# Expert pairs of a two-block transformer kernel: VectorE turns activations and places in 32x32 blocks, and three loads are issued at other times

## The chip, the cores and the metric

The kernel runs as one program on one core of one Trainium2 chip. The metric is the time of one execution on the device, in microseconds (us). The engines are PE (TensorE), DVE (VectorE), ACT (ScalarE), POOL (GpSimd) and SP (SyncE, which here only issues DMAs).

## The reference

Two transformer blocks run one after the other on 256 tokens of width 1024, all in fp32. The first has a convolution, a windowed attention and a gated delta rule side by side, then a hierarchical mixture of experts. The second has gated linear attention and block attention, then PEER, a lookup in tables of 16384 rows. The change is in the mixture of experts and in loads around it:

```python
pg = softmax(xt @ wg + bg); grp = argmax(pg)            # 4 groups of 8 experts
top_logit, top_e = top_k(el_grp, 2)                     # two experts of the group
gate = pg_top * softmax(top_logit)
...
def expert_block(args):
    xb, e = args
    return (silu(xb @ w1[e]) * (xb @ w3[e])) @ w2[e]    # w1, w3: 1024x512, w2: 512x1024
...
ys = ys * gate
return zeros_like(xt).at[tok].add(ys)
```

## The kernel before

**Expert weights.** The 32 experts are worked through in 16 pairs. A pair has six weight tiles of 2048 KB, which are two of w1, two of w3 and two of w2. All 96 tiles are read once, in this order, by DMAs that SP issues (`expert_tile`). Eight places hold them (`PLACES`): six slots of `ring` and two places called `beside`, each made of two halves of 1024 KB, three of the halves in `work` and one in `consts`. SP fills a place again when the semaphore `w_used` says that the matmuls on its old tile are over. PE raises `w_used` by two at the start of an "a" layer, a "b" layer and a gathering, so two places come free at each of these three points of a pair.

**A pair on PE.** Each expert takes at most 64 tokens (`CAP`), so the two experts of a pair share the 128 columns of PE's array. For pair p, PE runs:

- `first_layer(p, "a", 0)` (rows x w1) and `first_layer(p, "b", 2)` (rows x w3), 16 matmuls of 512 columns each
- `gathered(p + 1)`: the next pair's rows are picked out of `h_tok` with the 0/1 matrix `pm`
- "at": four PE transposes of `act_p` (silu(a)*b, rows by features), which DVE copies from PSUM to `actT`
- `scattered(p - 1)`: the last pair's result is added to its tokens through `pgT`
- "pt": two PE transposes of `pg`, the places times the gates, which DVE copies to `pgT`
- "y": `actT` x w2, in two halves of the width

**The order of banks.** `expert_jobs()` lists the PSUM results in the order in which PE makes them, with the engine that takes each. The class `Jobs` gives them the eight PSUM banks in turn, and a job waits until the result that lay in its bank before has been taken.

**Around the experts.** `na_out`, the output of the windowed attention, is in `work` at columns 15104 to 15615, inside the half `beside[0][1]` (13312 to 15359). So the four halves of the two `beside` tiles are issued after the matmuls "yT1" have read it. POOL loads `norm2_w`, the second block's second norm, into `mod[:, 0, :]` as the experts start. The first wait for a `w_used` in the loop over tiles stands here (`q` counts the tiles behind the first eight):

```python
with sp.Fori(0, 3) as i:
    for q in range(24):
        sp.wait_ge(w_used, i * 24 + (q + 3))
        expert_tile(i * 8 + (2 * ((8 + q) // 6) + q % 2), (8 + q) % 6, q % PLACES)
```

## Time and profile before

| | |
|---|---|
| three runs | 1512.1, 1512.28 and 1514.79 us, median 1512.28 |
| profiled execution, its span | 1512.7 us |
| PE busy | 1384.3 us, 92% |
| DVE busy | 788.9 us, 52% |
| ACT busy | 284.5 us, 19% |
| POOL busy | 325.9 us, 22% |
| moved by DMA | 551.35 MB, 364 GB/s on the mean |

The profile gives the profiled execution no other time than its span; it is 0.4 us above the median of the runs. Busy time of PE is time in which a matmul was under way, also when it was under way slowly. DMA share is the mean busy share of the 16 DMA engines, GB/s what they moved. In the timeline, the time in brackets behind a row is how long the engine sat idle before it, and what it waited for.

### The profile page before, as it was taken

The numbers are of one execution on the slowest core, as the hardware profiler recorded it, in microseconds if no ns is written. First come the engines' busy times: TensorE is split into PE (matmuls) and PEld (weight loads), VectorE is DVE, ScalarE is ACT, GpSimd is POOL, SyncE is SP. The second block draws the span as 40 slices with busy tenths as digits, with TensorE's granted clock in tenths as the row PEclk, the third lists the DMA queues.
The fourth block names the chain that finished last, engine by engine and source line by source line (L and its number), as shares of the span: only waits on it lengthen the run. The fifth ranks groups of instructions, "written<-read, shape, count | busy, mean of one in ns | idle before, by whom it ended". The sixth has DMA issues, their size and how long they took to land.

```text
span 1512.7 us, 16972 instructions
## 1 busy us (share of the span) xinstructions
PE 1384.3 (92%) x6354; PEld 721.6 (48%) x6354; DVE 788.9 (52%) x1912; ACT 284.5 (19%) x700; POOL 325.9 (22%) x315
## 2 busy tenths in 40 slices
PE   6999999999999999998999999997997877788787
PEld 4886665444444444443565755544453332333332
DVE  2257565232332332232534787757676666767555
ACT  1432313000000000000334433221212121212112
POOL 0001303000000000000000245444444443444451
PEclk9999999999999999999999999999999999998999
DMA  9743669999999999999343599999999999999997
GB/s 380 299 163 113 238 279 365 425 426 426 426 426 427 426 427 427 423 427 425 146 155 124 211 395 391 420 421 422 421 421 421 421 421 422 422 421 422 421 422 313
DMA packets 64579, 551.35 MB, mean 364 GB/s; under 512 B 9168, under 2 KB 9440, under 8 KB 11760
## 3 DMA queue, kind: packets, MB, share of 16 engines
q1 hardware_dynamic: 26080, 278.06, 44.5%
q0 software_dynamic: 38416, 272.17, 43.7%
q8 instruction: 53, 0.87, 0.2%
q14 instruction: 30, 0.25, 0.0%
HBM read 549.16 MB, written 1.05 MB: 364 GB/s over the span
## 4 chain that ended last, share of the span: by engine, by line
PE 62%; DMA 32%; issue 3%; DVE 1%; POOL 1%; ACT 1%; SPq 0%; POOLq 0%; DVEq 0%
DMA ring<-peer_uv_d,work 16%; PE ps L2051 12%; PE ps L1957 11%; PE ps L1299 7%; PE ps L2093 6%; DMA work<-peer_uv_d,work 5%; PE ps L1785 4%; DMA ring<-expert_w_d 4%; PE ps L1293 4%; PE ps L1746 3%; PE ps L2062 3%; PE ps L1614 2%; DMA consts_sb<-peer_uv_d,work 2%; DMA work<-expert_w_d 2%; DMA ring<-w_ada_d 2%
## 5 line engine op out<-in xcount | busy, mean ns | idle before, releaser
L1957 PE MATMUL ps<-ring,work 128*128 128x512 f32 x686 | 335.8, 631 | 73.0 <-ACT work L1230 71.8
L3281 DVE CUSTOM_DVE_ANT_0 ring<-ring,work 128x1024 f32<-128x1024 f32 x172 | 211.6, 1231 | 137.6 <-DMA ring<-peer_uv_d,work 136.3
L1957 PEld LDWEIGHTS ps<-ring,work 128*128 128x128 f32 x686 | 133.5, 201 | 253.7 <-issue 149.7
L2244 POOL DMA_INDIRECT ring<-peer_uv_d,work x170 | 187.9, 1105 | 231.3 <-PE ps L1957 206.5
L2051 PE MATMUL ps<-ring,work 128*64 128x512 f32 x768 | 168.1, 592 | 3.0 <-DMA ring<-expert_w_d 2.4
L1230 ACT ACTIVATE work<-consts_sb,work 128x128 f32<-128x128 f32 x256 | 85.2, 392 | 283.1 <-DVE work L3290 276.0
L1299 PE MATMUL ps<-ring,hT 128*128 128x512 f32 (+1 forms) x272 | 112.6, 569 | 1.8 <-DVE hT L3106 1.6
L2051 PEld LDWEIGHTS ps<-ring,work 128*64 128x64 f32 x768 | 57.0, 137 | 111.0 <-issue 111.0
L2824 DVE TENSOR_TENSOR work<-work,ps 128x512 f32<-128x512 f32 x16 | 11.0, 688 | 185.7 <-PE ps L2051 185.7
L2219 POOL DMA_DIRECT2D mod<-subkeys_d x1 | 0.5, 546 | 457.1 <-DVEq L2889 457.1
L1078 ACT ACTIVATE work<-ps 128x512 f32<-128x512 f32 x16 | 9.6, 597 | 430.6 <-PE ps L2051 430.6
L1957 PE MATMUL ps<-work 128*128 128x512 f32 x172 | 83.8, 614 | 4.6 <-ACT work L1230 4.6
L2093 PE MATMUL ps<-ring,work 128*64 128x512 f32 x384 | 85.0, 595 | 0.7 <-DVE work L2828 0.7
L1785 PEld LDWEIGHTS ps<-hT,ring 128*128 128x128 f32 x640 | 75.7, 192 | 13.0 <-issue 12.4
L1299 PEld LDWEIGHTS ps<-ring,hT 128*128 128x128 f32 x272 | 50.8, 190 | 56.5 <-issue 54.3
L1785 PE MATMUL ps<-hT,ring 128*128 128x128 f32 x640 | 76.5, 275 | 0.0
L2835 DVE TENSOR_TENSOR work<-ps,mod 128x512 f32<-128x512 f32 x32 | 22.1, 692 | 89.1 <-PE ps L2093 89.1
L3281 DVE CUSTOM_DVE_ANT_0 work<-work 128x1024 f32<-128x1024 f32 x43 | 52.7, 1225 | 27.4 <-DMA work<-peer_uv_d,work 27.1
L1746 PEld LDWEIGHTS ps<-work 128*128 128x128 f32 x512 | 58.4, 192 | 13.2 <-issue 13.2
L1957 PE MATMUL ps<-mod,work 128*128 128x512 f32 x80 | 43.8, 674 | 22.2 <-ACT work L1230 22.2
L1746 PE MATMUL ps<-work 128*128 128x128 f32 x512 | 61.4, 278 | 0.3 <-issue 0.3
L2062 PE MATMUL ps<-work 128*128 128x512 f32 x128 | 57.7, 593 | 0.8 <-DVE work L2835 0.8
(481 smaller groups left out, 1722.9 us busy)
## 6 DMA issues: line engine op xcount, KB each, us to landing
ring<-expert_w_d SPq DMA_DIRECT2D x72, 2048.0 KB, 19.3
work<-expert_w_d SPq DMA_DIRECT2D x36, 1024.0 KB, 18.6
ring<-w_ada_d SPq DMA_DIRECT2D x12, 2048.0 KB, 8.7
ring<-w_in_d SPq DMA_DIRECT2D x11, 2048.0 KB, 22.8
consts_sb<-expert_w_d SPq DMA_DIRECT2D x12, 1024.0 KB, 19.6
ring<-w_out_d SPq DMA_DIRECT2D x4, 2048.0 KB, 8.3
ring<-peer_w_query_d SPq DMA_DIRECT2D x4, 2048.0 KB, 7.7
ring<-w_in_d SPq DMA_DIRECT2D x4, 1024.0 KB, 29.8
```

The costliest lines, as they stand in the source:

```text
L1230: act.activation(diag[:, k % 4, :], ident, ACT.Copy, scale=w_cur[:, s, k:k + 1]).then_inc(diag_ready, 1)
L1293: last = pe.matmul(b[0:n, at:at + T], wt[:, k, c0:c0 + n], hT[:, k, :], start=(k == 0), stop=(k == KC - 1))
L1299: last = pe.matmul(b[:, at:at + n], hT[:, k, t * P:(t + 1) * P], wt[:, k, c0:c0 + n], start=(k == 0), stop=(k == KC - 1))
L1614: last = pe.matmul(ps[MID.bank(f"w{t}{n}")][:, :], mixT[k][:, t * P:(t + 1) * P], slot(N_HEAD - 2 + n)[:, k, :], start=(k == 0), stop=(k = ...
L1746: last = pe.matmul(b[:, c * P:(c + 1) * P], h_tok[:, t, k * P:(k + 1) * P], pm[:, t, :], start=(t == 0), stop=(t == TT - 1))
L1785: last = pe.matmul(b[0:n, at:at + P], wt[:, k, c0:c0 + n], hT[:, k, t * P:(t + 1) * P], start=(k == 0), stop=(k == KC - 1))
L1957: last = pe.matmul(ps[V_BANK[t] + n][:, :], diag[:, i % 4, :], v_row(i)[:, n * 512:(n + 1) * 512], start=(i % (16 * PH) == 0), stop=(i == ...
L2051: last = pe.matmul(b[u * CAP:(u + 1) * CAP, :], xeT[:, k, u * CAP:(u + 1) * CAP], wt[u](k), start=(k == 0), stop=(k == KC - 1), skip_group ...
L2062: pe.matmul(b[:, :], pgT[:, t, :], y_sb[:, n * 512:(n + 1) * 512], start=True, stop=True).then_inc(f_done, 1)
L2093: last = pe.matmul(b[u * CAP:(u + 1) * CAP, :], actT[:, c, u * CAP:(u + 1) * CAP], wt[u](c)[:, n * 512:(n + 1) * 512], start=(c == 0), sto ...
L2244: pool.indirect_dma_start(out=uv_rows(i), out_offset=None, in_=io["peer_uv"], in_offset=bass.IndirectOffsetOnAxis(ap=idx[:, s, k:k + 1], a ...
L3281: dve.tensor_tensor_reduce(out=u_row(i), in0=u_row(i), in1=h_tok[:, i // (16 * PH), :], scale=1.0, scalar=0.0, op0=ALU.mult, op1=ALU.add, ...
```

## The change

- For pairs 0 to 14 the PE transposes "at" and "pt" and the DVE copies behind them go. In their place DVE transposes from SBUF to SBUF, in blocks of 32x32: 16 instructions on 32 partitions by 4x32 elements turn `act_p` into `actT`, and 16 on 32 partitions by 2x32 turn `pg` into `pgT`. New semaphores `act_turned` and `pg_turned` count them; PE waits for the first ahead of "y", and for the second in the next pair's `scattered`. Pair 15 is as before.
- `Jobs` takes `passed`: six places in the turn of banks are passed over ahead of "a15", so that pair 15 and the second block have the banks that they had.
- `na_out` moves to columns 12288 to 12799 of `work`.
- Two of the four halves of the `beside` tiles are issued earlier, behind the load of `w_out` tile 0: one after "oT1", one after a count of `blk_next`.
- POOL issues the load of `norm2_w` after the experts, behind that of `subkeys`.

```diff
-    def __init__(self, jobs, ops=(), banks=8, apart=()):
+    def __init__(self, jobs, ops=(), banks=8, apart=(), passed=()):
         self.banks = banks
+        self.passed = dict(passed)
...
+        self.places, at = {}, 0
+        for name in self.turn:
+            at += self.passed.get(name, 0)
+            self.places[name] = at % banks
+            at += 1
...
     def before(self, name):
-        i = 0 if name in self.apart else self.turn.index(name)
-        return self.turn[i - self.banks] if i >= self.banks else None
+        if name in self.apart:
+            return None
+        same = [m for m in self.turn[:self.turn.index(name)] if self.places[m] == self.places[name]]
+        return same[-1] if same else None
...
-FAST = Jobs(expert_jobs())
+FAST = Jobs(expert_jobs(), passed=((f"a{PAIRS - 1}", 6),))
...
-        na_out = W(15104, 2, T)
+        na_out = W(12288, 2, T)
...
+            sp.wait_ge(hd, HEAD_AT["oT1"] + 1)
+            expert_tile(2, 0, RING, (1,))
+            sp.wait_ge(blk_next, len(CHAINS) * (LEVELS - 3))
+            expert_tile(3, 1, RING + 1, (0,))
             sp.wait_ge(hd, HEAD_AT["oB1"] + 1)
...
             for l in range(2):
-                expert_tile(2 + l, l, RING + l)
+                expert_tile(2 + l, l, RING + l, (l,))
...
                 def scattered(p):
                     taken(f"y{p}1")
+                    if p < PAIRS - 1:
+                        pe.wait_ge(pg_turned, 16 * (p + 1))
...
-                    taken(f"at{p}")
+                        taken(f"at{p}")
+                    else:
+                        pe.wait_ge(act_turned, 16 * (p + 1))
                     for n in range(2):
                         b = fbank(f"y{p}{n}")
...
-            pool.dma_start(mod[:, 0, :], io["norm2_w"].to_broadcast([P, D])).then_inc(in_nw3, 16)
...
             pool.dma_start(subT, io["subkeys"]).then_inc(in_sub, 16)
+            pool.dma_start(mod[:, 0, :], io["norm2_w"].to_broadcast([P, D])).then_inc(in_nw3, 16)
...
                     ftook(dve.tensor_tensor(act_p, sil, b[:, :], ALU.mult))
                     if p < PAIRS - 1:
+                        dve.wait_ge(f_d, FAST.taken(f"b{p}"))
+                        for u in range(4):
+                            for v in range(4):
+                                dve.transpose(actT[32 * v:32 * v + 32, :, 32 * u:32 * u + 32],
+                                              act_c[32 * u:32 * u + 32, :, 32 * v:32 * v + 32]).then_inc(act_turned, 1)
                         rows_in(p + 1)
-                    b = fjob(f"at{p}")
-                    ftook(dve.tensor_copy(actT.rearrange("p a b -> p (a b)"), b[:, :]))
+                    else:
+                        b = fjob(f"at{p}")
+                        ftook(dve.tensor_copy(actT.rearrange("p a b -> p (a b)"), b[:, :]))
                     if p:
                         added(p - 1)
-                    b = fjob(f"pt{p}")
-                    ftook(dve.tensor_copy(pgT.rearrange("p a b -> p (a b)"), b[:, 0:TT * P]))
+                    if p < PAIRS - 1:
+                        for u in range(4):
+                            for v in range(4):
+                                dve.transpose(pgT[32 * v:32 * v + 32, :, 32 * u:32 * u + 32],
+                                              pg[32 * u:32 * u + 32, p % 2, :, 32 * v:32 * v + 32]).then_inc(pg_turned, 1)
```

The order of DVE's instructions in pair 1, before: L2824 is the product silu(a)*b, L2805 the two copies of the next pair's rows, L2828 the copy of "at", L2814 the additions to `x`, L2832 the copy of "pt".

```order
276 L2824 TENSOR_TENSOR work<-work,ps 128x512 [waits sel_n,f_a,f_done]
277 L2805 COPY work<-ps 128x512 [waits f_done] x2
278 L2828 COPY work<-ps 128x512 [waits f_done]
279 L2814 TENSOR_TENSOR x<-x,ps 128x512 [waits f_done] x4
280 L2832 COPY work<-ps 128x256 [waits f_done]
```

The same place of the changed kernel, where L2847 is the product, L2827 the copies of rows, L2836 the additions and L2870 the two evictions of "y":

```order
277 L2847 TENSOR_TENSOR work<-work,ps 128x512 [waits sel_n,f_a,f_done]
278 L2852 STREAM_TRANSPOSE work<-work 32x4x32 [waits f_d]
279 L2852 STREAM_TRANSPOSE work<-work 32x4x32 x15
280 L2827 COPY work<-ps 128x512 [waits f_done] x2
281 L2836 TENSOR_TENSOR x<-x,ps 128x512 [waits f_done] x4
282 L2863 STREAM_TRANSPOSE work<-work 32x2x32 x16
283 L2870 TENSOR_TENSOR work<-ps,mod 128x512 [waits f_done] x2
```

The 16 transposes of the activations stand ahead of the copies of rows, where nothing stood; the two copies "at" and "pt" are gone.

The DMAs that SP issues between the attention and the first matmul of the experts, before:

```order
24 L813 DMA ring<-w_out_d 128x4096 [waits hd]
25 L806 DMA ring<-w_ada_d 128x4096 [waits gdn_done,hd]
26 L819 DMA ring<-expert_w_d 128x4096 x2
27 L822 DMA work<-expert_w_d 128x2048 [waits cond_moved,hd]
28 L822 DMA work<-expert_w_d 128x2048
29 L822 DMA consts_sb<-expert_w_d 128x2048
30 L822 DMA work<-expert_w_d 128x2048
31 L819 DMA ring<-expert_w_d 128x4096 [waits w_used] x2
32 L819 DMA ring<-expert_w_d 128x4096 [waits mid] x2
```

And in the changed kernel:

```order
24 L825 DMA ring<-w_out_d 128x4096 [waits hd]
25 L834 DMA work<-expert_w_d 128x2048 [waits hd]
26 L834 DMA consts_sb<-expert_w_d 128x2048 [waits blk_next]
27 L818 DMA ring<-w_ada_d 128x4096 [waits gdn_done,hd]
28 L831 DMA ring<-expert_w_d 128x4096 x2
29 L834 DMA work<-expert_w_d 128x2048 [waits cond_moved,hd]
30 L834 DMA work<-expert_w_d 128x2048
31 L831 DMA ring<-expert_w_d 128x4096 [waits w_used] x2
32 L831 DMA ring<-expert_w_d 128x4096 [waits mid] x2
```

Two halves stand ahead of the `w_ada` tile now, and two stay behind the first two expert tiles.

## Rows read from the trace of the kernel before

**Rows 1.** The page, busy tenths in 40 slices of 37.8 us
```profile
PE   6999999999999999998999999997997877788787
...
DMA  9743669999999999999343599999999999999997
GB/s 380 299 163 113 238 279 365 425 426 426 426 426 427 426 427 427 423 427 425 146 155 124 211 395 391 420 421 422 421 421 421 421 421 422 422 421 422 421 422 313
```

**Rows 2.** Chain of waits in one pair: start us, length us, engine and line
```profile
452.22 13.73 PE ps L2051 x64
465.96 3.77 PE ps L1746 x32
469.73 0.44 PE ps L2076 x4
470.16 3.44 PE ps L2062 x8
473.60 0.22 PE ps L2085 x2
473.82 7.02 PE ps L2093 x32
```

**Rows 3.** Windows around the experts, last columns PE clock, DMA share, GB/s
```profile
200.00:208.00 8.00, 8.00 (x52) 6.09 (x51) 6.05 (x10) 0.60 (x1) 0.00 (x0) 1.00 0.00 0
210.00:211.00 1.00, 1.00 (x4) 0.51 (x3) 0.93 (x1) 0.00 (x0) 0.00 (x0) 1.00 1.36 262
246.00:256.00 10.00, 9.22 (x62) 6.88 (x63) 7.09 (x31) 2.03 (x3) 6.02 (x12) 1.00 0.98 406
256.00:262.00 6.00, 6.00 (x30) 2.42 (x28) 1.62 (x8) 0.50 (x1) 1.38 (x3) 1.00 0.83 232
262.00:263.00 1.00, 1.00 (x7) 0.37 (x5) 0.00 (x0) 0.10 (x1) 0.00 (x0) 1.00 0.08 29
263.00:268.00 5.00, 5.00 (x26) 1.88 (x22) 0.00 (x0) 0.00 (x0) 0.00 (x0) 1.00 0.92 334
268.00:332.00 64.00, 63.27 (x330) 29.81 (x330) 20.55 (x43) 1.19 (x2) 0.00 (x0) 1.00 1.01 427
600.00:664.00 64.00, 62.17 (x306) 27.29 (x304) 17.54 (x38) 1.79 (x3) 0.00 (x0) 1.00 1.01 425
```

**Rows 4.** Timeline of PE, rows ahead of which it sat idle
```profile
631.76 7.09 PE L2051 MATMUL ps<-ring,work 128*64 128x512 f32 x32 [0.68 <-DMA ring<-expert_w_d]
...
661.63 0.61 PE L2051 MATMUL ps<-work 128*64 128x512 f32 x1 [1.04 <-DMA work<-expert_w_d]
...
692.21 7.09 PE L2051 MATMUL ps<-ring,work 128*64 128x512 f32 x32 [1.75 <-DMA ring<-expert_w_d]
...
718.44 13.97 PE L1299 MATMUL ps<-ring,hT 128*128 128x512 f32 x32 [1.61 <-DVE hT L3106]
```

**Rows 5.** Timeline of SP's DMA issues, as the experts start
```profile
245.94 0.33 SPq L819 DMA_DIRECT2D ring<-expert_w_d  x1
...
262.49 7.13 SPq L819 DMA_DIRECT2D ring<-expert_w_d  x4
...
281.60 0.95 SPq L819 DMA_DIRECT2D ring<-expert_w_d  x2
```

**Rows 6.** DVE's groups by form: count, busy us, mean ns
```profile
L2426 DVE STREAM_TRANSPOSE ring<-ring 128x256 f32<-128x256 f32 x20 | 8.7, 441 | 0.6
...
L2515 DVE STREAM_TRANSPOSE ring<-ring 32x128 f32<-32x128 f32 x2 | 0.6, 301 | 0.1
```

**Rows 7.** Timeline of DVE and PE, start of the experts, and pair 0's "y"
```profile
253.54 1.29 DVE L2805 COPY work<-ps 128x512 f32<-128x512 f32 x2 [1.05 <-issue]
...
254.37 13.95 PE L2051 MATMUL ps<-ring,work 128*64 128x512 f32 x64 [0.51 <-DVE work L2805]
...
273.48 1.94 PE L2093 MATMUL ps<-ring,work 128*64 128x512 f32 x8 [0.73 <-DVE work L2828]
```

**Rows 8.** DVE's reader of the moved norm row (L3122)
```profile
L3122 DVE SCALAR_TENSOR_TENSOR work<-x,small,mod x1: 1285/1285/1285, 834.3 to 834.3; 128x1024 f32<-128x1024 f32 x1
```

More of the change, by code:

```diff
@@ L238, in __init__ @@
         assert len(self.at) == len(jobs)
+        self.places, at = {}, 0
[3 more added lines that the diff above has]
+            at += 1
     def bank(self, name):
-        return self.apart[name] if name in self.apart else self.turn.index(name) % self.banks
+        return self.apart[name] if name in self.apart else self.places[name]
     def done(self, name):
@@ L262, in expert_jobs @@
             jobs += [(f"g{p + 1}0", "D"), (f"g{p + 1}1", "D")]
-        jobs.append((f"at{p}", "D"))
+        if p == PAIRS - 1:
+            jobs.append((f"at{p}", "D"))
         if p:
             jobs += [(f"sc{p - 1}{n}", "D") for n in range(4)]
-        jobs.append((f"pt{p}", "D"))
+        if p == PAIRS - 1:
+            jobs.append((f"pt{p}", "D"))
         jobs += [(f"y{p}0", "D"), (f"y{p}1", "D")]
@@ L681, in two_blocks @@
         pg_ready = sem("pg_ready")
+        act_turned = sem("act_turned")
+        pg_turned = sem("pg_turned")
         cond_moved = sem("cond_moved")
@@ L813, in _, with expert_tile @@
             sp.dma_start(ring[:, 1, :], io["w_out"][0, :, :]).then_inc(head_landed[1], 16)
-            def expert_tile(e, l, place):
+            def expert_tile(e, l, place, pieces=range(2)):
                 v = io[("expert_w1", "expert_w3", "expert_w2")[l // 2]]
@@ L820, in expert_tile @@
                 else:
-                    for c in range(2):
+                    for c in pieces:
                         sp.dma_start(beside[place - RING][c], v[e, :, c * 2048:(c + 1) * 2048])\
                             .then_inc(beside_landed[place - RING], 16)
+            sp.wait_ge(hd, HEAD_AT["oT1"] + 1)
+            expert_tile(2, 0, RING, (1,))
+            sp.wait_ge(blk_next, len(CHAINS) * (LEVELS - 3))
+            expert_tile(3, 1, RING + 1, (0,))
             sp.wait_ge(hd, HEAD_AT["oB1"] + 1)
@@ L2072, in _ @@
                         gathered(p + 1)
-                    b = fbank(f"at{p}")
-                    taken(f"b{p}")
-                    for c in range(4):
-                        last = pe.transpose(b[:, c * P:(c + 1) * P], act_p[:, c * P:(c + 1) * P], ident)
-                        if c == 0 and p == PAIRS - 1:
-                            last.then_inc(w_used, 2)
-                    last.then_inc(f_done, 1)
+                    if p == PAIRS - 1:
+                        b = fbank(f"at{p}")
+                        taken(f"b{p}")
+                        for c in range(4):
+                            last = pe.transpose(b[:, c * P:(c + 1) * P], act_p[:, c * P:(c + 1) * P], ident)
+                            if c == 0:
+                                last.then_inc(w_used, 2)
+                        last.then_inc(f_done, 1)
                     if p:
                         scattered(p - 1)
-                    b = fbank(f"pt{p}")
-                    pe.wait_ge(pg_ready, p + 1)
-                    for t in range(TT):
-                        last = pe.transpose(b[:, t * P:(t + 1) * P], pg[:, p % 2, t, :], ident)
-                    last.then_inc(f_done, 1)
-                    taken(f"at{p}")
+                    if p == PAIRS - 1:
+                        b = fbank(f"pt{p}")
+                        pe.wait_ge(pg_ready, p + 1)
+                        for t in range(TT):
+                            last = pe.transpose(b[:, t * P:(t + 1) * P], pg[:, p % 2, t, :], ident)
+                        last.then_inc(f_done, 1)
+                        taken(f"at{p}")
+                    else:
+                        pe.wait_ge(act_turned, 16 * (p + 1))
                     for n in range(2):
@@ L2825, in _ @@
                     if p < PAIRS - 1:
+                        dve.wait_ge(f_d, FAST.taken(f"b{p}"))
[3 more added lines that the diff above has]
+                                              act_c[32 * u:32 * u + 32, :, 32 * v:32 * v + 32]).then_inc(act_turned, 1)
                         rows_in(p + 1)
-                    b = fjob(f"at{p}")
-                    ftook(dve.tensor_copy(actT.rearrange("p a b -> p (a b)"), b[:, :]))
+                    else:
+                        b = fjob(f"at{p}")
+                        ftook(dve.tensor_copy(actT.rearrange("p a b -> p (a b)"), b[:, :]))
                     if p:
                         added(p - 1)
-                    b = fjob(f"pt{p}")
-                    ftook(dve.tensor_copy(pgT.rearrange("p a b -> p (a b)"), b[:, 0:TT * P]))
+                    if p < PAIRS - 1:
[3 more added lines that the diff above has]
+                                              pg[32 * u:32 * u + 32, p % 2, :, 32 * v:32 * v + 32]).then_inc(pg_turned, 1)
+                    else:
+                        b = fjob(f"pt{p}")
+                        ftook(dve.tensor_copy(pgT.rearrange("p a b -> p (a b)"), b[:, 0:TT * P]))
                     for n2 in range(2):
```

1 line of the change is left out of this document (added).

## The prediction

> **What bounds the kernel now.** I read the 40 slices of the page first. From the slice that begins at 265 us to the one that ends near 718 us both PE and DMA are at nine tenths or more, and DMA moves 423 to 427 GB/s in each [rows 1]. Two engines look like the bound, and only one of them can be. So I went to the chain of waits. It runs through PE alone for most of the stage: in one pair 13.73 us for "a" and "b" (L2051), 3.77 for the next pair's rows (L1746), 0.44 for "at" (L2076), 3.44 for the scatter (L2062), 0.22 for "pt" (L2085) and 7.02 for "y" (L2093), together 28.62 us [rows 2]. By this view PE sets the pace.
>
> The windows say something else. A pair's six tiles are 6 x 2048 KB = 12.58 MB. PE asks for that every 28.6 us, which would be 440 GB/s. DMA delivered 427 GB/s just after the start (268 to 332) and 425 late in the stage (600 to 664), at a share of 1.01 both times [rows 3], so 29.5 us for a pair. The rate is the same early, with few tiles waiting, and late, with many. So it is a ceiling, and the stream falls 0.9 us further behind PE in each pair. PE doesn't feel it at first, because eight tiles were loaded ahead. It feels it at the end: it waits 0.68, 1.04 and 1.75 us for expert tiles, one of the waits a pair, at 631, 661 and 692 us [rows 4]. The last two are the steady difference of 0.9 us and a bit, with the lead used up. So the end of the stage is set by the arrival of the last w3 tile at 692, and from there the way is fixed: "b", the rest of pair 15 and the first matmul of the second block at 718.44 [rows 4], some 26.2 us later.
>
> When does the stream start? SP issues the eighth tile at 245.94 and the ninth only at 262.49, when PE has begun "b" of pair 0 and frees the first two places [rows 5]. In between the stream runs dry: 406 GB/s up to 256, 232 up to 262, and 29 in the microsecond from 262 to 263 [rows 3]. Whatever happened before, the last 88 tiles start there.
>
> **The change part by part.**
>
> *PE transposes of 15 pairs.* They remove 0.44 + 0.22 = 0.66 us of a pair on PE [rows 2], 9.9 us in all. PE then needs 27.96 us a pair and the stream still 29.5. The freed time turns into waits for tiles. The lead at pair 1 was about 12 x 0.93 - 0.68 = 10.5 us (twelve pairs until the first wait), and it is now used up at 1.6 us a pair, after six or seven pairs, at some 450 us instead of 631. From there each pair has one wait of about 1.6 us, ahead of "b". On the end this is worth 0. The cover is the stream; if it went away, 9.9 us would be gained.
>
> *DVE's 32 transposes a pair.* The nearest row is the same form in this kernel: 32 partitions by 128 elements took 301 ns, and 128x256 took 441 [rows 6]. 128 elements more cost 140 ns, so 64 fewer should cost 70 less, 0.23 us for the form of "pt". If each runs alone, it is 16 x 0.30 = 4.8 us for `actT` and 16 x 0.23 = 3.7 us for `pgT`. Two copies of 0.69 in a row took 1.29 us [rows 7], so successive instructions overlap by about 0.09 us, which gives 16 x 0.21 = 3.4 us and 2.3 us. I take the overlap. `actT` is needed when PE has done rows and scatter, 3.77 + 3.44 = 7.2 us after "b" [rows 2]; DVE is through 0.7 + 3.4 = 4.1 us after it, or 5.5 at the upper price. The copies of rows are then late by 3.4 to 4.8 us, and who waits for them is the next "a", which starts 7.2 + 7.0 = 14.2 us after "b". `pgT` is needed only in the next pair's scatter. The two evictions of "y" stand behind its 16 transposes on DVE: these begin when the scatter's sums are added, about 8 us after "b", and end by 10.3 to 11.8, and the halves of "y" are ready at 10.7 and 14.2. That may delay the first eviction by a microsecond, and nothing reads it before the next pair. Cost 0.
>
> The Trainium skill speaks against this part: "VectorE: DVE Perf Modes" (The three transpose paths; Rules for kernel authors) gives a 128x128 transpose to TensorE where PSUM will do as destination, and has VectorE at 311 ns for one pass of 32x32 blocks. At that figure 16 passes would be an estimated 5.0 us, which is still inside the 7.2 us, so the sum is the same by page and by row.
>
> *Pair 0.* It has no scatter, so its "y" waits: before for the two DVE copies, 0.73 us, until 273.48 [rows 7]. "b" ends at 268.4, so after the change "y" can start at 268.4 + 0.7 + 3.4 = 272.5, or 273.9 at the upper price. This moves the release at 281.60 [rows 5] by -1.0 to +0.4 us. At this release the four tiles issued at 262.49 and behind are nearly through: 8.4 MB less the 1.7 MB moved up to 268, at 427 GB/s, last until 283.8. A new tile needs about a microsecond to start, so no hole opens at either end. Worth 0, with -0.3 as the worst case of a hole.
>
> *The early halves.* They take 2.1 MB, 4.9 us at 426 GB/s, out of the busy stretch before 256 and put it where DMA moved nothing at all (200 to 208) [rows 3]. Both waits are over by then, so SP isn't held up ahead of the `w_ada` tile. But the number of places stays eight. The first eight tiles are in at 251 instead of 256, and the stream stands dry for 11 us instead of 6, until PE frees a place at 262.49. Bytes leave a stretch whose end nobody waits for. Worth 0 directly.
>
> *The norm's row.* Its 0.5 MB (1.2 us of stream) were issued at 255.7 and were over before 262, where only 29 GB/s moved [rows 3]. They filled the dry stretch. Their removal saves 0; at the upper end they and the other small loads slowed the ramp of 263 to 268, which ran at 334 instead of 426 GB/s: 5 x 92 / 426 = 1.1 us, most of which any start needs (262 GB/s in the first full microsecond of the start at 209.3 [rows 3]). I take 0.1 of 0 to 0.5. After the experts the row is read first at 834.3 [rows 8], 116 us after its new issue at 717, so its place behind `subkeys` costs 0.
>
> *A small gain by way of the start.* Ahead of the first copies of rows DVE sits idle for 1.05 us at 253, put down to issue, at the branch into the experts' code [rows 7], with the stream at 406 GB/s [rows 3]. If this is a fetch that stands behind the stream, it gets shorter, now that the stream is dry at 251. PE starts that much earlier, frees the places earlier, and all 88 tiles move along. Bounds 0 and 1.05; I take 0.4, because nothing shows that the stream is its cause. `na_out` and the bank order cost 0: pair 15 and the second block keep their banks, and in the other pairs "a" takes the bank of rows whose copy it needs in any case.
>
> **Sum.** -0.4 - 0.1 = -0.5 us against 1512.7 us of the profiled execution. It stands 0.4 us above the median of the runs, 1512.28, so the runs should show 1511.8. A change under 0.2% (3 us) can't be told from none in this kernel.
>
> **Rivals.**
>
> 1. *The stream gets shorter by what left it.* If the dry stretch were no real gap, 2.1 + 0.5 MB less would end it 4.9 + 1.2 = 6.1 us earlier: 1506.2. For it: DMA's share is 0.98 up to 256 and 0.83 to 262. Against it: 29 GB/s at 262, and the issue gap of 16.5 us.
> 2. *PE's time is kept.* If PE is the bound as the chain has it, 9.9 us are gained: 1502.4; with all three waits gone too, 1499. For it: only 3.5 us of waits for tiles. Against it: 440 GB/s would be needed, and no window shows more than 427 over 64 us.
> 3. *Slower: DVE is late for "y".* If a block transpose here takes t, `actT` is ready 0.7 + 16 t after "b". Above t = 0.41 us PE waits in every pair; the stream's slack of 1.6 us a pair hides this until t = 0.51. At 0.6 a pair takes 27.96 + 3.1 = 31.1 us, 1.5 us over the stream, and once the lead is used up the kernel is at some 1525. Against it: 301 ns in the same form [rows 6].
>
> **How the numbers follow.** The forecast, within 3 us of before, gets 0.68 and has its own range of 1510 to 1514 (bounds -1.9 and +0.3 and the spread of the runs). Rival 1 gets 0.12, rival 2 0.06, rival 3 0.08, and 0.06 is for what I don't see, mostly small. The range takes in the forecast and rival 1, 0.8 together: 1505.8 to 1514.6. Faster 0.2, same 0.7, slower 0.1.
>
> **What the changed profile would show.** The idle time of L2051's successor for expert tiles rises from 3.5 us to about 13, in steps of about 1.6 us a pair from some 450 us on. The ninth tile's issue stays within 1 us of 262.5. The last wait ends within 1 us of 692. DVE's 16 transposes take 3.4 to 4.8 us and PE doesn't wait for them outside pair 0. The windows from 268 to 700 stay at 425 to 427 GB/s. The prediction is wrong if the stream runs faster than 427, if the ninth tile is issued much earlier, or if PE waits for DVE ahead of "y" in each pair.

## The result, and the profile after

The changed kernel takes 1515.97 us on the median of 10 runs (1514.55 to 1518.43), and the kernel before 1512.36 us on the median of 10 beside it (1511.72 to 1514.79). The ratio is 1.0021, with a 95% interval of 1.0013 to 1.0029. So the change costs about 3.6 us, some 0.2%. The forecast was 0.5 us less than before. The sign was wrong, and the time lies above the range.

The page of the changed kernel, engines and slices:

```profile
PE 1373.1 (91%) x6264; PEld 710.5 (47%) x6264; DVE 896.7 (59%) x2362; ACT 284.8 (19%) x700; POOL 321.6 (21%) x315
...
PE   7999999999999999999999999897987777677787
...
DMA  9743788999999999999343599999999999999997
GB/s 380 300 161 113 266 333 295 403 426 426 426 426 426 427 426 426 425 427 425 152 156 122 213 399 389 420 422 421 421 421 420 422 421 422 421 422 421 422 421 301
...
q14 instruction: 33, 0.27, 0.0%
```

PE's busy time fell by 11.2 us and DVE's rose by 107.8, and the stream still runs at 425 to 427 GB/s, as in [rows 1]. But the slice that begins at 265 us shows 403 GB/s, where before showed 425. Something is missing at the start. (The last line is needed further down.)

The timeline of PE, rows ahead of which it sat idle or of pair 0, from "b" of pair 0 to the second block:

```profile
252.13 13.95 PE L2067 MATMUL ps<-ring,work 128*64 128x512 f32 x64 [0.47 <-DVE work L2827]
...
266.02 3.84 PE L1762 MATMUL ps<-work 128*128 128x128 f32 x32
272.22 8.78 PE L2115 MATMUL ps<-ring,work 128*64 128x512 f32 x32 [2.36 <-DVE work L2852]
...
483.93 7.09 PE L2067 MATMUL ps<-ring,work 128*64 128x512 f32 x32 [0.38 <-DMA ring<-expert_w_d]
514.41 8.78 PE L2067 MATMUL ps<-ring,work 128*64 128x512 f32 x32 [2.31 <-DMA ring<-expert_w_d]
574.32 7.09 PE L2067 MATMUL ps<-ring,work 128*64 128x512 f32 x32 [2.08 <-DMA ring<-expert_w_d]
603.79 7.09 PE L2067 MATMUL ps<-ring,work 128*64 128x512 f32 x32 [1.30 <-DMA ring<-expert_w_d]
634.28 8.78 PE L2067 MATMUL ps<-ring,work 128*64 128x512 f32 x32 [2.31 <-DMA ring<-expert_w_d]
685.92 7.09 PE L2067 MATMUL ps<-ring,work 128*64 128x512 f32 x32 [0.68 <-issue]
693.17 7.09 PE L2067 MATMUL ps<-ring,work 128*64 128x512 f32 x32 [0.16 <-issue]
...
719.01 3.24 PE L1315 MATMUL ps<-ring,hT 128*128 128x512 f32 x7 [1.21 <-DVE hT L3141]
```

The later rows are what was predicted: waits for tiles from some 484 us on, instead of only from 631 [rows 4]. The third row was not. PE waits 2.36 us for the transposes in pair 0, against 0.73 for the copy of before [rows 7], and then the same 32 matmuls take 8.78 us instead of 7.09.

PE began the experts here at 252.13 us, and in the profile of before at 254.37 [rows 7], and the two spans are only 1.6 us apart (1514.3 and 1512.7). That is because the two profiled executions don't stand at the same place among the runs. In the changed kernel and in every run below, a span is 1.7 to 2.6 us shorter than the same execution's time among the runs (1514.3 and 1516.07 for the changed kernel, whose median is 1515.97). With that added, the 1512.7 us of before fit only the slowest of its first three runs, 1514.79 us, which is 2.4 above the median, and not 0.4 as the text ahead and the prediction have it. The start of the experts goes with this: in the four other kernels whose profile has it at 254.2 us or later, that execution took 0.9 to 1.9 us more than the kernel's median, and in the four with a start before 252.5 us it was between 0.8 under the median and 0.1 above. The start thus differs from execution to execution (251.9 to 254.6 us over all profiles), and with one profile of each kernel it can't be charged to the change. I leave it out and count from the first expert matmul to the first matmul of the second block. That was 718.44 - 254.37 = 464.07 us before and 719.01 - 252.13 = 466.88 after, 2.8 more. From there to the end of the span it is 794.3 and 795.3 us, 1.0 more. Together that is 3.8, near the 3.6 us between the medians.

DVE in pair 0, and SP's issues there:

```profile
266.13 0.69 DVE L2847 TENSOR_TENSOR work<-work,ps 128x512 f32<-128x512 f32 x1 [10.59 <-PE ps L2067]
266.85 5.31 DVE L2852 STREAM_TRANSPOSE work<-work 32x128 f32<-32x128 f32 x16
272.19 1.29 DVE L2827 COPY work<-ps 128x512 f32<-128x512 f32 x2
273.51 4.25 DVE L2863 STREAM_TRANSPOSE work<-work 32x64 f32<-32x64 f32 x16
```

```profile
260.25 0.97 SPq L831 DMA_DIRECT2D ring<-expert_w_d  x2
...
282.04 0.95 SPq L831 DMA_DIRECT2D ring<-expert_w_d  x2
```

Sixteen transposes take 5.31 us, 0.33 each. From the ninth tile's issue to the release by pair 0's "y" it is 282.04 - 260.25 = 21.79 us, and was 281.60 - 262.49 = 19.11 [rows 5]. The release is 2.7 us late: 1.63 of longer idle, 1.69 of slower matmuls, less the 0.66 of PE transposes that went.

Windows of the changed kernel (columns as in [rows 3]):

```profile
200.00:208.00 8.00, 8.00 (x43) 5.44 (x42) 5.57 (x10) 0.00 (x0) 0.00 (x0) 1.00 0.19 71
...
256.00:262.00 6.00, 6.00 (x30) 2.42 (x28) 0.00 (x0) 0.60 (x1) 1.15 (x2) 1.00 0.46 130
...
263.00:268.00 5.00, 5.00 (x33) 2.91 (x30) 1.75 (x5) 0.00 (x0) 0.00 (x0) 1.00 0.98 416
268.00:272.00 4.00, 1.86 (x17) 1.67 (x15) 3.62 (x13) 0.00 (x0) 0.00 (x0) 1.00 1.03 434
272.00:274.00 2.00, 1.78 (x6) 0.68 (x8) 1.91 (x5) 0.00 (x0) 0.00 (x0) 0.64 0.99 426
274.00:276.00 2.00, 2.00 (x6) 0.48 (x4) 1.75 (x9) 0.00 (x0) 0.00 (x0) 0.51 1.03 442
276.00:280.00 4.00, 4.00 (x22) 1.32 (x20) 2.26 (x8) 0.00 (x0) 0.00 (x0) 1.00 1.01 430
280.00:282.00 2.00, 2.00 (x12) 0.69 (x10) 0.95 (x4) 0.00 (x0) 0.00 (x0) 1.00 0.67 287
282.00:284.00 2.00, 2.00 (x12) 0.72 (x10) 1.37 (x7) 0.00 (x0) 0.00 (x0) 1.00 0.71 164
```

The clock column falls to 0.64 and 0.51 behind the idle time, which is the 1.2 GHz level, and is back at 1.00 (2.4 GHz) from 276 on. At 280 to 284 the stream of expert tiles has a hole: 287 and 164 GB/s instead of 426, so (139 + 262) x 2 / 426 = 1.9 us of stream are gone. Before, the same windows moved 467 and 434:

```profile
280.00:282.00 2.00, 2.00 (x12) 0.69 (x10) 1.34 (x5) 0.00 (x0) 0.00 (x0) 1.00 1.09 467
282.00:284.00 2.00, 2.00 (x12) 0.72 (x10) 0.98 (x4) 0.00 (x0) 0.00 (x0) 1.00 1.02 434
```

That is 1.9 of the 2.8 us in this trace. The rest had to be found by experiments.

### The profile page after: what moved, and what is told of

Same layout as the page of the kernel before. It is cut to its first block, busy times and chain, and to the rows that moved or that the text cites. A ratio compares the mean times of both kernels' runs of the same rounds, so it can differ in the third digit from the quotient of the medians.

```text
span 1514.3 us, 17213 instructions
## 1 busy us (share of the span) xinstructions
PE 1373.1 (91%) x6264; PEld 710.5 (47%) x6264; DVE 896.7 (59%) x2362; ACT 284.8 (19%) x700; POOL 321.6 (21%) x315
## 4 chain that ended last, share of the span: by engine, by line
PE 58%; DMA 36%; issue 3%; DVE 2%; ACT 1%; POOL 1%; SPq 0%; POOLq 0%; DVEq 0%
DMA ring<-peer_uv_d,work 16%; PE ps L2067 11%; PE ps L1973 10%; DMA ring<-expert_w_d 9%; PE ps L1315 7%; DMA work<-peer_uv_d,work 7%; PE ps L2115 5%; PE ps L1801 4%; PE ps L1309 4%; PE ps L2080 3%; PE ps L1762 2%; PE ps L1630 2%; DMA consts_sb<-peer_uv_d,work 2%; PE ps L1323 2%; DMA mod<-peer_uv_d,work 2%
## 5 line engine op out<-in xcount | busy, mean ns | idle before, releaser
L2067 PE MATMUL ps<-ring,work 128*64 128x512 f32 x768 | 172.0, 602 | 9.7 <-DMA ring<-expert_w_d 8.4
L2847 DVE TENSOR_TENSOR work<-work,ps 128x512 f32<-128x512 f32 x16 | 11.0, 688 | 189.3 <-PE ps L2067 189.3
L2067 PEld LDWEIGHTS ps<-ring,work 128*64 128x64 f32 x768 | 59.4, 139 | 119.5 <-issue 119.5
L2115 PE MATMUL ps<-ring,work 128*64 128x512 f32 x384 | 86.7, 605 | 2.4 <-DVE work L2852 2.4
L2852 DVE STREAM_TRANSPOSE work<-work 32x128 f32<-32x128 f32 x240 | 72.7, 303 | 7.6
L2863 DVE STREAM_TRANSPOSE work<-work 32x64 f32<-32x64 f32 x240 | 56.6, 236 | 7.1
```

The lines of the kernel that those rows point to most:

```text
L2067: last = pe.matmul(b[u * CAP:(u + 1) * CAP, :], xeT[:, k, u * CAP:(u + 1) * CAP], wt[u](k), start=(k == 0), stop=(k == KC - 1), skip_group ...
L2115: last = pe.matmul(b[u * CAP:(u + 1) * CAP, :], actT[:, c, u * CAP:(u + 1) * CAP], wt[u](c)[:, n * 512:(n + 1) * 512], start=(c == 0), sto ...
L2852: dve.transpose(actT[32 * v:32 * v + 32, :, 32 * u:32 * u + 32], act_c[32 * u:32 * u + 32, :, 32 * v:32 * v + 32]).then_inc(act_turned, 1)
```

## The experiments

Every ratio is to the kernel before, run beside it on the same chip. Each kernel had 11 runs, but 7 for the one with 900 memsets, and 10 and 4 for the two with a lighter stream. Each has one trace. From the first expert matmul to the second block, the three kernels whose stage should be alike (before, loads alone, 120 wide memsets) have 464.07, 463.88 and 463.70 us, so a difference of 0.4 us between two traces says nothing.

### Which part costs: turns alone, loads alone

The first run has the changed kernel with the loads and `na_out` put back; the second has the kernel before with only the loads and `na_out` moved.

```diff
 # turns alone, against the changed kernel (the norm's row goes back too)
-            expert_tile(2, 0, RING, (1,))
-            expert_tile(3, 1, RING + 1, (0,))
...
-                expert_tile(2 + l, l, RING + l, (l,))
+                expert_tile(2 + l, l, RING + l)
```

> The changed kernel with all loads where the kernel before has them (the early halves, the norm's row and na_out undone). Theory A (pair 0's 'y' starts late, its release comes late, a hole opens in the stream of expert tiles): the whole loss stays, ratio to before 1.0015 to 1.003, with a dip in the DMA rate near 280 to 284 us and a 'y' of pair 0 that takes over 8 us. Theory B (the moved loads cost the time): ratio within 0.0007 of 1.

> The kernel before with the moved loads alone (early halves, norm's row after the experts, na_out at 12288), PE transposes in all pairs. Theory A (pair 0's late release): within 0.0007 of 1, since the eight places are full before PE frees the first in any case. Theory B (the moved loads cost the time): 1.0015 to 1.003. A gain of 6 us by a shorter stream would be 0.996.

Turns alone: 1516.09 us, ratio 1.0019 (1.0010 to 1.0028). Loads alone: 1513.41 us, 1.0001 (0.9991 to 1.0010). The loads are worth nothing either way, as predicted; whatever costs is in the turns. The gain of 0.4 by way of the start doesn't show: with loads alone PE began the experts at 254.62 us, as late as before.

One part of what was expected of turns alone did not come. "y" of pair 0 waits as long as in the changed kernel, but runs at full speed, and the granted clock stays at 1.00:

```profile
272.97 7.09 PE L2111 MATMUL ps<-ring,work 128*64 128x512 f32 x32 [2.36 <-DVE work L2848]
```

So in this trace the release comes 1.0 us late, counted from the first expert matmul, and not 2.7 (281.09 - 252.89 = 28.20 us, against 27.23 before and 29.91 in the changed kernel). The stage takes 465.84 us, 1.8 more than before's and 1.0 less than the changed kernel's. So the same wait comes with the slow clock in some traces (the changed kernel, and its version with a lighter stream) and without it in this one. Whether that goes by the execution or by the moved loads, and how often it comes, no run here tells.

### Pair 0: by PE, and with PE kept busy

In the first kernel pair 0 is turned by PE like pair 15. In the second it is turned by DVE, and PE gets nine matmuls without use ahead of "y" (they are fp32, and each fp32 matmul has two rows in the trace, so 18).

```diff
 # pair 0 by PE: ON_PE = (0, 15), used wherever the last pair was asked for
-                    if p == PAIRS - 1:
+                    if p in ON_PE:
                         b = fbank(f"at{p}")
```

```diff
 # pair 0 by DVE, PE kept busy
+                    if p == 0:
+                        warm(9, FAST.bank("y00"))
                     if p == PAIRS - 1:
                         b = fbank(f"at{p}")
```

> The changed kernel, but pair 0 is turned by PE as before (as pair 15 is). Theory A (the loss is made in pair 0): the loss is gone, ratio 0.999 to 1.0007, the last wait for a w3 tile ends about 429.7 us after the ninth tile's issue as in the kernel before (433.0 in the changed one), and PE's waits for tiles add up to 9 us or more. Theory C (waits for tiles lower PE's clock late in the stage and cost the time there): the loss stays, 1.0015 or more.

> The changed kernel with nine 128x128 matmuls on the identity, results unused, ahead of pair 0's wait for the block transposes. They fill the 2.4 us in which PE sat idle. If the clock after that idle time is a part of the loss (y of pair 0 took 8.78 us instead of 7.02), y takes 7.0 us again and 1.7 us of the hole close: ratio 1.0005 to 1.0015. If only the wait counts, the ratio stays at 1.002.

Pair 0 by PE: 1515.37 us, 1.0016 (1.0007 to 1.0025). PE kept busy: 1515.11 us, 1.0011 (1.0002 to 1.0020). The timeline of the second, PE in pair 0:

```profile
271.26 2.17 PE L1329 MATMUL ps<-consts_sb 128*128 128x128 f32 x18
273.79 2.80 PE L2117 MATMUL ps<-ring,work 128*64 128x512 f32 x12 [0.35 <-DVE work L2854]
```

Its idle time is 0.35 us, "y" takes 7.09 again and the clock doesn't fall. With pair 0 by PE the windows from 280 to 284 are back at 426 GB/s. With PE kept busy "y" starts no earlier (20.08 us behind the first expert matmul, 20.09 in the changed kernel), so only the slow clock is taken away, and the release is 1.0 us late as in turns alone. From first expert matmul to second block these two take 465.15 and 465.27 us, 1.6 to 1.7 less than the changed kernel's 466.88, and 1.1 to 1.2 more than before's 464.07. So the traces show the mechanism in pair 0. Where the clock fell (changed kernel) it costs 1.7 us against pair 0 by PE, and 1.6 of them go when PE is kept busy. Where it didn't fall, a release 1.0 us late costs 0.1 us (PE kept busy) or 0.7 (turns alone, 465.84), near what two traces can't tell apart. The medians of the runs put it at 0.7 to 1.0 us (turns alone 1516.09, against 1515.37 with pair 0 by PE and 1515.11 with PE kept busy, on the same chip), but the intervals of 1.0019, 1.0016 and 1.0011 overlap, so the runs alone don't prove it. For pair 0 by PE the expectation, 0.999 to 1.0007, was missed: most of the loss stays. Pair 0 isn't the whole.

### Without a dry stretch and without pair 0

Here SP loads the first six tiles behind the eighth in halves, the first half as soon as that half of its place is free (pair 0's "y" runs over `c` outermost for it), so the stream starts earlier. Once it stands on the kernel before, and once on the changed kernel with pair 0 turned by PE.

```diff
+                if q < 6 and q % 2 == 0:
+                    sp.wait_ge(h_ready, 5 + q // 2 + 1)
+                    for m in range(2):
+                        half_of_tile(e + m, l + m, q + m, 0, part_landed[q // 2])
                 sp.wait_ge(w_used, q + 3)
+                if q < 6:
+                    half_of_tile(e, l, q, 1, landed[(N_HEAD + q) % RING])
```

> The kernel before, with the first six weight tiles of its places given back in halves: PE tells SP half way through 'a', 'b' and 'y' of pair 0 (where 'y' runs over its four row chunks outermost), and SP loads half a tile then, the other half where the whole tile was loaded. All computed results are the reference's. If the start of the stream at 262.5 us sets the end of the stage, the ninth and tenth tile's first halves are issued at 259, 3.5 us earlier, the last w3 tile lands up to 3.5 us earlier, PE's waits for tiles (3.5 us) go nearly to nothing: ratio 0.9975 to 0.9985. If PE is the bound: within 0.0005 of 1.

> The changed kernel with pair 0 turned by PE, and with the first six tiles given back in halves as in the kernel halves_before. The stream starts 3.5 us earlier and PE has time to spare: the last w3 tile 3.5 us earlier than with pair 0 on PE alone, ratio 0.9985 to 0.9998 (1.0016 less 0.0023). If it is as fast as halves_before or faster, VectorE's block transposes are worth something once the stream starts early; theory D says that it is slower by 0.001.

On the kernel before: 1511.40 us, 0.9992 (0.9982 to 1.0001). On the changed kernel: 1513.09 us, 1.0000 (0.9991 to 1.0009). The windows of the first show that the stream starts earlier (308 and 418 GB/s, where [rows 3] have 232 and 29):

```profile
256.00:262.00 6.00, 6.00 (x31) 2.42 (x28) 0.61 (x3) 0.60 (x1) 1.15 (x2) 1.00 0.84 308
262.00:263.00 1.00, 1.00 (x7) 0.34 (x4) 0.00 (x0) 0.00 (x0) 0.00 (x0) 1.00 1.00 418
```

The stage is 1.7 us shorter for it (462.37 against 464.07). That is the way which a bound by the stream asks for, but half the size that was expected: counted from the first expert matmul, the ninth tile's issue comes 3.6 us earlier (257.73 - 253.22, against 262.49 - 254.37), PE's waits for tiles fall from 3.5 us only to 2.0, and the ratio, whose interval takes in 1, isn't the 0.9975 to 0.9985 of the expectation. And again the kernel with DVE's turns is the slower one of the two by its median, 1513.09 against 1511.40 us (the intervals overlap) and by its trace, 462.89 against 462.37, though its pair 0 is as before and its stream has no hole from 268 on. In it PE waits 11.0 us for tiles.

### What DVE's instructions do to the stream

Each tile is landed by 16 signals, one for each part of it. I took from the trace how far apart the 16 lie, for each ring tile between 250 and 700 us, and beside it the times of the 8 KB packets of the page's queue q14 ("instruction"):

```
                    spread of the 16 landings, us              q14 packets at, us
before              1.85 to 429, 3.4 from 474, 4.96 at 692     293, 349, 492, 614, 630
changed kernel      2.33 to 429, 3.28 from 435, 4.24 at 494,   294, 299, 362, 432, 489, 562,
                    5.27 at 564, 6.2 from 629, 6.28 at 693     615, 622
```

In the changed kernel the packets at 432, 489, 562 and 622 are each followed within 7 us by a tile whose parts land 0.8 to 1.0 us further apart, and the distance isn't made up again. In the kernel before, the packets at 492 and 614 leave no step. The two large steps there, at 474 and 677, come right behind packets of 16 KB on the other instruction queue, q8 (472 and 672), whose number is nearly the same in both kernels (53 and 52 on the page); the other 13 of these packets from 300 us on leave no step of more than 0.4 us. So not every packet shows, which it need not where it meets a part that isn't the last. A tile counts when its last part has landed. So I formed a theory (called the fetch theory below): DVE's instructions are fetched in blocks by one of the DMA engines; all 16 are kept full by the tiles, so each fetch sets that one engine back, and the tile is as late as its slowest part. The count fits: the 8 KB packets on this queue are 30 in the run before and 33 in the run after, which has 450 more instructions on DVE.

The Trainium skill has two things that bear on this. "DMA: Bandwidth & Descriptors" (Queues, rings and completion order) has a queue row of the runtime's own, for refills among other things, on the same DMA engines, which take turns between their rows packet by packet; "Vector Engine (DVE) Microarchitecture Reference" (Instruction fetch and dispatch) has 64 bytes to an instruction, which makes an estimated 128 to a packet of 8 KB. The runs below agree with the second: 900 instructions added 7 packets, 129 to each.

The first test adds 450 memsets of one column to the kernel before, and nothing else. The second has DVE turn only the activations (pairs 1 to 14), and leaves `pg` to PE.

```diff
+                    if p < PAIRS - 1:
+                        for m in range(30):
+                            dve.memset(grT[:, m:m + 1], 0.0).then_inc(sel_n, 1)
```

> The kernel before with 30 one-column memsets on VectorE at the end of each of pairs 0 to 14 (450, as many instructions as the change adds there), in time in which VectorE is idle; nothing else changes. Theory D (the added instructions must be fetched by the DMA engines that carry the full stream; one engine falls behind, and each tile lands when the last engine has moved its part): three more 8 KB fetches in the stage, the 16 parts of the last expert tiles land 6 us or more apart instead of 5, the last w3 tile comes some 1 us later, ratio 1.0007 to 1.0015. Rival: VectorE has half its time free, so the ratio stays within 0.0005 of 1.

> The changed kernel with only the activations turned by VectorE, in pairs 1 to 14; the places in all pairs, and all of pairs 0 and 15, by PE. It adds 15 x 14 = 210 instructions to VectorE instead of 450. Theory D (fetches of instructions): ratio 1.0003 to 1.001, between the kernel before and the one that keeps only pair 0 on PE (1.0016). Rival (the waits of PE for tiles, and its clock after them): as that kernel, 1.0013 or more, since PE waits nearly as long.

The memsets: 1514.37 us, 1.0009 (1.0000 to 1.0018). Activations alone: 1513.35 us, 1.0005 (0.9996 to 1.0014). Both lie where the theory wants them and neither is clear of no change. In the trace of activations alone the two large steps, of 1.6 and 1.7 us, again follow 16 KB packets, and no 8 KB packet leaves one. So I tested the dose, and the busy time by itself: 900 such memsets, and 120 wide ones (8 a pair of 128x256, each waiting for the last).

```diff
-                        for m in range(30):
-                            dve.memset(grT[:, m:m + 1], 0.0).then_inc(sel_n, 1)
+                        for m in range(8):
+                            dve.wait_ge(sel_n, fn[0])
+                            dve.memset(grT[:, 0:T], 0.0).then_inc(sel_n, 1)
```

> The kernel before, with 60 memsets of one column added on DVE behind the additions of each of the pairs 0 to 14 (900 in all, about 3.6 us of DVE in a pair that has some 15 us to spare). The run with half as many gave 1.0009. Fetch theory (each block of DVE instructions is fetched by one DMA engine that the expert tiles keep full, so the 16 parts of a tile land further apart): more fetches than the 8 of that run between the first expert matmul and 692 us, the parts of the last w3 tile 6 to 8 us apart instead of 4.96, ratio 1.0012 to 1.0025. Rival, that the 0.0009 was noise or the exact place of one fetch: 0.9995 to 1.0010, with no wider spread than 6.2 us.

> The kernel before, with 8 memsets of 128x256 on DVE behind the additions of each of the pairs 0 to 14: 120 instructions in all, each waits for the one before. It keeps DVE busy for some 2 to 3 us in a pair, longer than the 30 one-column memsets did, with a quarter of the instructions. Fetch theory: about the fetches of before (5 or 6), spread of the last w3 tile 5.0 to 5.5 us, ratio 0.9995 to 1.0005. Rival, that it is DVE's activity in itself (its access to SBUF beside the DMA writes and the matmuls' reads): 1.0009 or more.

900 memsets: 1518.18 us, 1.0034 (1.0022 to 1.0045). 120 wide ones: 1513.49 us, 1.0004 (0.9995 to 1.0013). The groups of DVE and the q14 line of the page for the wide ones:

```profile
L2840 DVE MEMSET work<- 128x256 f32 x120 | 32.6, 272 | 12.6
...
q14 instruction: 30, 0.25, 0.0%
```

And for the 900, with rows of PE's timeline:

```profile
L2839 DVE MEMSET work<- 128x1 f32 x900 | 21.2, 59 | 0.1
...
q14 instruction: 37, 0.30, 0.0%
...
637.09 7.09 PE L2051 MATMUL ps<-ring,work 128*64 128x512 f32 x32 [1.66 <-DMA ring<-expert_w_d]
...
666.62 0.61 PE L2051 MATMUL ps<-work 128*64 128x512 f32 x1 [0.70 <-DMA work<-expert_w_d]
...
696.99 7.09 PE L2051 MATMUL ps<-ring,work 128*64 128x512 f32 x32 [1.53 <-DMA ring<-expert_w_d]
```

This separates the number of instructions from busy time. The 900 narrow memsets keep DVE busy for 21.2 us, the 120 wide ones for 32.6, and it is the narrow ones that cost, more than the 1.0012 to 1.0025 expected. PE waits for neither. PE starts the experts at 254.37 us in both kernels, the 900 and before, and its last wait ends at 696.99 instead of 692.21 [rows 4], 4.8 us later. The spread grows by as much:

```
                        q14 packets   of them between the    spread at the    first expert matmul
                        on the page   first expert matmul    last w3 tile     to second block
                                      and 692 us             us               us
before                  30            5                      4.96             464.07
loads alone             30            5                      4.86             463.88
120 wide memsets        30            6                      4.93             463.70
activations alone       31            6                      5.50             464.20
450 narrow memsets      33            8                      6.21             464.66
900 narrow memsets      37            12                     9.89             468.83
pair 0 by PE            34            8                      6.27             465.15
turns alone             33            8                      6.50             465.84
changed kernel          33            8                      6.28             466.88
```

The stage grows as the spread does: by 4.76 us where the spread grows by 4.93, for seven fetches more. For three more it is 1.3 us in the spread and 0.6 to 1.1 in the time, with pair 0 as before. In the trace with 900 memsets the growth from 350 us on is made in eight steps of 0.7 to 1.0 us, and each stands at the first ring tile that lands behind an 8 KB packet (at 372, 427, 458, 513, 544, 598, 634 and 686 us); the packet at 618 leaves none, and there is no other step above 0.3. So it is shown that 900 short instructions cost 5 us without anybody waiting for them, by way of the slowest part of a tile and in steps that follow the instruction packets. Three things stay open. A packet takes only 0.31 to 0.33 us in most records, and why it costs three times that isn't shown, since the records don't say which DMA engine it went through. The cost of three and of seven isn't in proportion. And each added instruction also raises a semaphore; no run has the one without the other, so only the time of the steps speaks for the fetches.

### Was PE's time really there?

The last two kernels load only three quarters of each expert tile that goes to the ring, from the seventh on. A part of the weights is left out, and the matmuls run as before on what lies there.

```diff
-                    sp.dma_start(ring[:, sl, :], v[e, :, :]).then_inc(landed[sl], 16)
+                    cols = 4096 if first_tiles[0] < 6 else 3072
+                    first_tiles[0] += 1
+                    sp.dma_start(ring[:, sl, 0:cols], v[e, :, 0:cols]).then_inc(landed[sl], 16)
```

> The kernel before, in which each expert tile that goes to the ring, from the seventh issue on, loads only 3072 of its 4096 columns, so a part of the weights is left out (the matmuls run as before on what lies there). A pair then needs 10.5 MB where two of its tiles are in beside and 9.4 MB otherwise, 22 to 25 us at 427 GB/s, less than PE's 28.6. If the stream bounds the stage and PE is just behind: PE waits for no tile, and the 3.5 us of waits are gone, ratio 0.997 to 0.9985.

> The changed kernel with the same three quarters of each ring tile loaded, so a part of the weights is left out. If the stream is what hides the 9.9 us that PE gave up: they appear now, less the late start of pair 0's y and its slow clock (2 to 3 us), so this kernel is 6 to 9 us below light_before, ratio to the kernel before 0.991 to 0.9945. Rival, that DVE's turns hold PE up in each pair whatever the stream does, or that the PE transposes cost nothing in the first place: within 3 us of light_before.

With a lighter stream the kernel before takes 1508.46 us, 0.9975 (0.9966 to 0.9984), and the changed one 1502.76 us, 0.9933 (0.9918 to 0.9948). Neither has a wait for a tile left. The changed one is 5.7 us faster now, just under the 6 to 9 expected; in the traces the stage takes 453.60 us against 459.61, 6.0 less. That is the 9.9 us of PE transposes, less pair 0's 3.3 us (2.35 idle instead of 0.72, and 8.78 instead of 7.09) and a wait of 0.67 at 673 us that is put down to issue. So the work that the change takes from PE is real, and it is the stream that hides it.

## Why the prediction was wrong, and where it was right

**Right: the stream is the bound, and PE's 9.9 us turn into waits.** PE waits 8.4 us for tiles ahead of L2067 and loses 3.4 more to the slower clock behind two of these waits, 11.8 together where 13 was forecast; with pair 0 by PE it is 13.0 us of waits for tiles. They began at 484 us, where 450 was forecast. Two were longer than forecast (2.31 us instead of 1.6), and it is behind these that the clock fell (8.78 us at 514.41 and 634.28); the stream hid this. Rival 2 is out, and the lighter stream shows what it would have been worth. The windows stayed at 426 GB/s, and rival 1 is out: loads alone are worth 0.0001.

**Wrong, the larger part: pair 0, "Worth 0, with -0.3 as the worst case of a hole".** The transposes were put at 0.21 us each, with 0.30 as the upper price, and measured 0.333 from start to start. The overlap that I took from two copies of 128x512 [rows 7] isn't there; the records have 0.303 us for one, and a gap of 0.03 behind it. So DVE needs 5.3 us, above the upper end of 4.8, and "y" starts 6.1 us after "b" ends (4.1 to 5.5 forecast). That is 0.6 us beyond the upper end. So the release moves by +1.0 us by the wait alone (turns alone, trace with the clock at 1.00), where -1.0 to +0.4 stood. What the prediction had no term for is the next step: in the changed kernel's trace PE runs at the 1.2 GHz level for a while after its 2.36 us without work, "y" takes 1.69 us longer, and the release moves by +2.7 us. By the prediction's own figures the slack was about 1.2 us (tiles under way until 283.8, release at 281.60, a microsecond for a new tile to start). A delay of 2.7 is larger, and a hole of 1.9 us opens in a stream that never catches up. The overlap that fails is the first step, the clock behind the wait the second, and most of the cost hangs on the second: 1.7 us in the trace where the clock fell, 0.1 and 0.7 in the two where it didn't. Of rival 3's mechanism only this one place came true: in pairs 1 to 14 rows and scatter cover 7.2 us, and the transposes take 5.3.

**Wrong, the other part: "DVE's 32 transposes a pair ... Cost 0".** The sum over DVE's time was right: nobody waits for it there. What was missing is a price for their number. 450 instructions more on DVE come with three instruction packets more, in a stage whose stream keeps the DMA share at 1.01. With pair 0 out of the way (pair 0 by PE, 420 instructions more) the stage is 465.15 - 464.07 = 1.1 us longer; the 450 memsets alone gave 0.6.

**The sum.** 1.7 us for pair 0, 1.1 for the number of instructions, 1.0 behind the stage: 3.8 by the traces, against 3.6 between the medians. For turns alone it is 0.7, 1.1 and 0.8: 2.6, against 2.9 between its medians. That the sums come out is partly luck: each trace is one execution, and how often the clock falls in pair 0 over the ten isn't known. The last 1.0 isn't explained. From the first matmul of the second block to the end it is 794.1 to 794.8 us in six of the seven kernels without DVE's turns and 795.0 to 795.5 in the seven with them, but the kernel with 450 memsets has 795.5 and that with 900 has 794.7, so the number of instructions alone doesn't set it. Where the instruction blocks of the second block begin relative to its own transfers, which fill the DMA engines again, could do it; that was only thought, not tried.

**The term for the start** (-0.4) and the one for the norm's row (-0.1) were too small to be seen. The profiles start the experts at 251.9 to 254.6 us, by the execution that was profiled; the prediction took one profile's 254.37 for a fixed number. So the ninth tile's issue, expected within 1 us of 262.5, stands at 260.25 in the changed kernel's trace.

**The range** failed because its upper end, 1514.6, had next to no cost in it: no edit had been given a price above nothing, and the one bound for a hole (0.3 us) was worked out from a price (0.30 a transpose) that had no margin over the record of a single instruction.

## What to carry to other kernels

When work is moved to an engine that has time to spare, first ask how many instructions it becomes. Here 32 short ones replaced 6 on PE and 2 on DVE; they cost about 0.03 us each over their own duration, and by their mere number they set back a transfer stream that was the bound, in pairs where nobody waited for the engine.

Where a stream of tiles is the bound, treat every release at its start as part of the bound: a few microseconds of delay in the first pair, where only four tiles are in flight, were not regained here, while 9.9 us of PE's time in fifteen pairs were worth nothing. And a new idle time on PE should be priced twice, with and without slower matmuls behind it: here waits of 2.15 to 2.36 us made the matmuls behind them 1.7 us longer in six places and left them as they were in others.

To see whether a freed microsecond is real, lighten the presumed bound and compare the two kernels again: 5.7 us appeared at once.

## What the runs showed of the hardware that I had not expected

- The 16 parts of a tile drift apart in a saturated stream, mostly in steps of 0.7 to 1.2 us that follow single instruction packets of 8 KB, and here and there one of 16 KB. From some 350 us to the end of the stage the distance isn't made up: 1.85 us at 429 and 4.96 at 692 in the kernel before, 9.89 at 697 with 900 more instructions.
- A STREAM_TRANSPOSE of 32 partitions by 128 fp32 elements shows 303 ns and starts every 333; one by 64 shows 236 and starts every 265 (56.6 us busy and 7.1 idle over 240). The next doesn't begin before the one ahead of it has ended.
- The length of an idle time doesn't decide whether PE's clock falls to the 1.2 GHz level. 32 matmuls of 512 columns took 8.78 us instead of 7.09 behind idle times of 2.36 and 2.31 us (twice) in the changed kernel, 2.35 with the lighter stream, 2.17 us in turns alone (at 573.94) and 2.15 with PE kept busy (at 574.28). They took 7.09 behind 2.36, 2.30 and 2.21 us in turns alone, 2.16 with PE kept busy (at 634.27), 2.29 with pair 0 by PE (at 602.88), and 2.62 in activations alone (at 690.27). Behind 2.09 us and less it never fell in these stages.
